# Two-block transformer kernel: the masks of the attention scores added by one fp32r product of 256 columns a head instead of two fp32 products of 128

## The chip, the cores and the metric

The kernel runs on one core of a Trainium2 chip. The metric is the device time of that core in microseconds (us): the median of three runs for the kernel before. A core has five engines that run their own instruction streams and meet only at semaphores: TensorE (PE, matrix products into PSUM), VectorE (DVE), ScalarE (ACT), GpSimd (POOL) and SyncE (SP, which here only issues transfers). A product on PE is two instructions in the trace: the load of the stationary operand (LDWEIGHTS, shown as engine PEld) and the product itself (MATMUL, engine PE). A product of fp32 operands is recorded as two such pairs, one of fp32r operands as one pair.

## The reference, cut to what matters

Two models follow each other on one sequence of 256 tokens of width 1024. The first has two layers; each layer projects the tokens, splits the result over four mixers (MoBA, MLA, stick-breaking, Mamba-2), adds the mixed heads through `w_out`, and ends in a convolved gated feed-forward. The second has four layers, which the change does not touch. All is fp32.

Three of the four mixers of a layer need a mask on a 256x256 table of scores per head, four heads each:

```
# MoBA (one block of 256) and MLA: softmax over the keys up to the query
s = einsum("bqhd,bkhd->bhqk", q, k) * scale
s = where(kpos <= qpos, s, -inf);  p = softmax(s)
# stick-breaking: strictly earlier keys
z = einsum("bqhd,bkhd->bhqk", q, k) * scale
strict = kpos < qpos
log_1mb = where(strict, log_sigmoid(-z), 0)
a = where(strict, exp(log_sigmoid(z) + reverse_cumsum(log_1mb) - log_1mb), 0)
```

With queries and keys in blocks of 128 a head has three blocks of scores that matter; two of them lie on the diagonal and take the mask, the third is whole. 12 heads a layer over 2 layers make 24 heads with two masked blocks each.

## The kernel before, in words

**Precision.** Every large product (weights times features) is taken apart into fp32r halves: a weight chunk lands in `raw` by DMA (1 MB each, issued by SP at L499), ACT writes its high part `whi` (`split`, ACT at L1171), DVE its low part `wlo` (L1658), and PE does three fp32r products per tile (L677 to L679 in the projection of the first model, L723 to L725 and L792 elsewhere). A ring of five slots holds the chunks; a slot's next transfer waits for `chunk_done`, which PE signals when it has used the chunk five back. The small products of the mixers are fp32, as they are.

**The mixers.** `Tensor.mix` (called once a layer) is PE's program, written out by hand: it weaves the projection's chunks, `chunk(0)` to `chunk(10)`, with the small products of the mixers, so that ACT and DVE can work on one mixer while PE multiplies weights. The places in it that matter here, in order: `stick_scores(0)`, `chunk(6)`, `stick_scores(1)` (after waiting for `expo`, which DVE signals at L2205), the transposes at L998, `stick_tail(0)`, `chunk(7)`, `turn_mla(0)`, `stick_tail(1)`, `chunk(8)`, `turn_mla(1)`, `chunk(9)`, `causal_scores("mla", 0)`, transposes at L1026, `causal_scores("mla", 1)`, `chunk(10)`, `causal_scores("moba", 0)` and `("moba", 1)`, the Gram products at L1042 and L1043, and then the value products up to the output projection at L792. ACT and DVE have matching programs named `mix`, also in a fixed order.

**The scores.** `stick_scores(k)` does two heads, `causal_scores(kind, i, bank)` two heads. Each head has a bank of PSUM with 384 columns: block (0,0) in columns 0:128, and the row of the second query block. In `stick_scores` the layout is (0,0), (0,1), (1,1) with the transposed scores, so its two masked blocks are columns 0:128 and 256:384; in `causal_scores` it is (0,0), (1,0), (1,1), masked at the same places. A head is four fp32 products: one of 128 columns, one of 256, and two of 128 in which the identity multiplies a table of zeros and -1e30 from `consts` (`strict_add`, `causal`) and adds it to the block. Stick-breaking and MoBA heads are 64 wide, so query and key occupy 64 partitions (the even head partitions 0:64, the odd head 64:128) and their products use 64 rows of the array; MLA heads are 96 wide and use 96. The mask products use all 128. The trace names a tensor by the memory it lies in: `sb_t` and `moba_t` appear as `xn`, `mla_t` as `proj`.

**DVE before the first mixers.** In layer 0 DVE computes the rotary angles (L1676 to L1708) and builds a bias table (`extend_bias`, L1668) between two weight splits, after waiting for `tables_in`, the transfer that brings the masks among other constants.

Of the kernel before, what the change touches and what calls it, by code (L numbers as in the profile page):

```python
# [26 lines left out]
F32R = mybir.dt.float32r  # L27
# [4 lines left out]
P = 128  # L32
SEQ, D, FF = 256, 1024, 2816
# [41 lines left out]
def constants():  # L75

    parts, at = [], 0

    def add(name, a):
        nonlocal at  # L80
        a = np.asarray(a, np.float32)
        parts.append(a)
        CONST[name] = (at, at + a.shape[1])
        at += a.shape[1]

    r, c = np.arange(P)[:, None], np.arange(P)[None, :]
    add("ident", r == c)
    add("minus_half", np.full((P, 24), -0.5))
    for name, dim in (("inv64", HD), ("inv32", ROPE)):
        inv = np.float32(1) / (np.float32(THETA) ** (np.arange(0, dim, 2, dtype=np.float32) / np.float32(dim)))  # L90
        add(name, np.broadcast_to(inv.astype(np.float32), (P, dim // 2)))
    add("upto", r <= c)
    add("ones", np.ones((P, P)))
    add("causal", np.where(c <= r, 0, BIG))
    add("upto_add", np.where(r <= c, 0, BIG))
    add("strict_add", np.where(r < c, 0, BIG))
    add("from_neg", -(r >= c).astype(np.float32))
    add("ones_neg", -np.ones((P, P)))
    add("dist", -np.abs(np.arange(P)[:, None] + np.arange(SEQ)[None, :] - 127))
    return np.concatenate(parts, 1)  # L100
# [25 lines left out]
class Semaphores:  # L126


    def __init__(self, new):
        self.params_in = new("params_in")  # L130
        self.tables_in = new("tables_in")
        self.rows_in = new("rows_in")
        self.rows_cleared = new("rows_cleared")
        self.rows_turned = new("rows_turned")
# [140 lines left out]
def view(t, **k):  # L275
    return t.rearrange("p (a b) -> p a b", **k)
# [314 lines left out]
class Tensor(Program):  # L591
# [342 lines left out]
    def mix(self, l):  # L934

        e, m, s = self.e, self.m, self.s
        ps, proj, ident = m.ps, m.proj, m.ident
        r = self.round("mixers")
# [13 lines left out]
        for t in range(TT):  # L952
            e.transpose(ps[:, 2, t * P:(t + 1) * P], m.cn[:, t, 0:P], ident)
            e.transpose(ps[0:64, 2, 256 + t * P:256 + (t + 1) * P], m.cn[:, t, P:QR], ident)
            ins = e.transpose(ps[:, 3, t * P:(t + 1) * P], m.cn[:, t, QR:QR + KVR], ident)
# [12 lines left out]
        for x in range(2):  # L968
            for j in range(2):
                for t in range(TT):  # L970
                    col = C_SB + x * GROUP + j * P
                    ins = e.transpose(ps[:, 2 + x, j * 256 + t * P:j * 256 + (t + 1) * P], proj[:, t, col:col + P], ident)
# [10 lines left out]
        for t in range(TT):  # L983
            ins = e.matmul(ps[:, 6, t * 4:t * 4 + 4], m.upto, m.a[:, t, :], start=True, stop=True)
        ins.then_inc(s.cum_done, 1)

        e.wait_ge(s.sb_kept, r)
        self.stick_scores(0)
        chunk(6)

# [96 lines left out]
    def stick_scores(self, k):  # L1087

        e, m = self.e, self.m
        for h in (2 * k, 2 * k + 1):  # L1090
            part, out = slice(64 * (h % 2), 64 * (h % 2) + 64), m.ps[:, 2 + 4 * k + h % 2, :]
            e.matmul(out[:, 0:SEQ], m.sb_t[part, 2 + h // 2, 0:P], m.sb_t[part, h // 2, :], start=True, stop=True)
            e.matmul(out[:, 0:P], m.ident, m.cst("strict_add"), start=False, stop=True, skip_group_check=True)
            e.matmul(out[:, SEQ:SEQ + P], m.sb_t[part, 2 + h // 2, P:SEQ], m.sb_t[part, h // 2, P:SEQ], start=False, stop=True,
                     skip_group_check=True)
            ins = e.matmul(out[:, SEQ:SEQ + P], m.ident, m.cst("strict_add"), start=False, stop=True, skip_group_check=True)
        ins.then_inc(self.s.z_done, 1)

    def stick_tail(self, k):

# [17 lines left out]
    def causal_scores(self, kind, i, bank):  # L1118

        e, m = self.e, self.m  # L1120
        q, k, _ = m.heads[kind]
        for h in range(2):
            out = m.ps[:, bank + h, :]
            e.matmul(out[:, 0:P], q(i, h, 0), k(i, h, 1), start=True, stop=False)
            e.matmul(out[:, 0:P], m.ident, m.cst("causal"), start=False, stop=True)
            e.matmul(out[:, P:3 * P], q(i, h, 1), k(i, h, 2), start=True, stop=True)
            ins = e.matmul(out[:, 2 * P:3 * P], m.ident, m.cst("causal"), start=False, stop=True, skip_group_check=True)
        ins.then_inc(self.s.scores, 1)

    def turn_pair(self, n, bank):  # L1130
# [512 lines left out]
class Vector(Program):  # L1643
# [488 lines left out]
    def mix(self, l):  # L2132
# [41 lines left out]
        if l == 0:  # L2174
            self.rotary_angles()
            e.wait_ge(s.tables_in, 16)
            self.extend_bias()
        self.split(5, 0)

# [462 lines left out]
def build(nc, d):  # L2642
    with ExitStack() as ctx:
        m = Memory()

        def sb(stack, name, shape, dt=F32):
            return stack.enter_context(nc.sbuf_tensor(name, shape, dt))
# [4 lines left out]
        m.xn = sb(ctx, "xn", [P, TT, D])  # L2652
        m.consts = sb(ctx, "consts", [P, CONST["dist"][0]])
        m.cols = sb(ctx, "cols", [P, ROW_TILES * P])
        m.trig = sb(ctx, "trig", [P, 192])
        m.ss = sb(ctx, "ss", [P, 2])
        m.ms = sb(ctx, "ms", [P, 2])
# [4 lines left out]
        m.rs2 = sb(ctx, "rs2", [P, 2])  # L2662
        m.st = sb(ctx, "st", [P, 60])
        m.lam_d = sb(ctx, "lam_d", [P, 4])
        m.ahead = sb(ctx, "ahead", [P, 4])
        m.pos = sb(ctx, "pos", [P, 2])
        m.pos_i = sb(ctx, "pos_i", [P, 2], I32)
        m.negmax = sb(ctx, "negmax", [P, 4, 2, 2])
# [76 lines left out]
        m.ident = m.consts[:, CONST["ident"][0]:CONST["ident"][1]]  # L2745
        m.upto = m.consts[:, CONST["upto"][0]:CONST["upto"][1]]
        m.ones = m.consts[:, CONST["ones"][0]:CONST["ones"][1]]
        m.cst = lambda n: m.consts[:, CONST[n][0]:CONST[n][1]]
        m.wide_ = lambda n: m.wide[:, WIDE[n][0]:WIDE[n][1]]
        m.row_loads = len(row_pieces())  # L2750
# [76 lines left out]
```

## Time and profile before

| | before |
|---|---|
| median of 3 runs | 2723.49 us (2721.34 to 2723.83) |
| profiled execution, its own time | 2722.85 us |
| its span, first to last instruction | 2721.1 us |
| mean granted TensorE clock | 0.983 of full speed |
| PE busy | 2628.8 us (97%), 18629 products |
| DVE busy | 1696.3 us (62%) |
| ACT busy | 1317.5 us (48%) |

The span is what the trace covers; 1.75 us of the execution's own time lie around it. A busy share is an average over stages with different limits, and a matmul's recorded duration contains the time it takes to come out of the array, so two products whose records overlap follow each other more closely than their durations say: what a product costs in a row of products is the distance between starts. The stages that the change touches are the mixers of the two layers of the first model, at about 64 to 138 us and 408 to 482 us of the span.

### The profile page before, as it was taken

The numbers are of one execution on the slowest core, as the hardware profiler recorded it, in microseconds if no ns is written. First come the engines' busy times: TensorE is split into PE (matmuls) and PEld (weight loads), VectorE is DVE, ScalarE is ACT, GpSimd is POOL, SyncE is SP. The second block draws the span as 40 slices with busy tenths as digits, with TensorE's granted clock in tenths as the row PEclk, the third lists the DMA queues.
The fourth block names the chain that finished last, engine by engine and source line by source line (L and its number), as shares of the span: only waits on it lengthen the run. The fifth ranks groups of instructions, "written<-read, shape, count | busy, mean of one in ns | idle before, by whom it ended". The sixth has DMA issues, their size and how long they took to land.

```text
span 2721.1 us, 43386 instructions
## 1 busy us (share of the span) xinstructions
PE 2628.8 (97%) x18629; PEld 2440.0 (90%) x18629; DVE 1696.3 (62%) x2201; ACT 1317.5 (48%) x1932; POOL 150.7 (6%) x228
## 2 busy tenths in 40 slices
PE   7989999999999999999998999999889999999999
PEld 7979889898998889989988998998879899888997
DVE  5668657686665656647656665655766566565763
ACT  5746457465443445445444544444454454344542
POOL 2010001000000100000010000001010000010000
PEclk9999999999999999999999999999999999998999
DMA  7256542475765637657654766765356566562763
GB/s 209 80 142 187 189 146 94 124 186 186 188 191 171 194 93 194 186 172 204 190 190 136 209 186 180 194 191 183 119 134 187 188 182 189 179 194 94 193 187 124
DMA packets 568280, 460.19 MB, mean 169 GB/s; under 512 B 12314, under 2 KB 529258, under 8 KB 568090
## 3 DMA queue, kind: packets, MB, share of 16 engines
q1 hardware_dynamic: 562643, 441.88, 55.7%
q0 software_dynamic: 4656, 15.30, 1.9%
q8 instruction: 147, 2.41, 0.4%
q10 hardware_dynamic: 791, 0.25, 0.1%
q14 instruction: 43, 0.35, 0.0%
HBM read 456.30 MB, written 1.10 MB: 168 GB/s over the span
## 4 chain that ended last, share of the span: by engine, by line
PE 87%; DVE 4%; DMA 3%; ACT 3%; issue 1%; POOL 1%; SPq 0%; DVEq 0%; POOLq 0%; ACTq 0%
PE ps L792 27%; PE ps L723 15%; PE ps L724 15%; PE ps L725 15%; PE ps L677 3%; PE ps L679 3%; PE ps L678 3%; PE ps L619 1%; DMA raw<-in_a_w_qkv 1%; ACT whi L1171 1%; DVE wlo L1658 1%; ACT h_hi L1171 1%; DMA raw<-in_w_in 1%; DMA raw<-in_ffn_w_in 1%; DVE h_lo L1719 1%
## 5 line engine op out<-in xcount | busy, mean ns | idle before, releaser
L1658 DVE TENSOR_TENSOR wlo<-raw,whi 128x2048 fp32r<-128x2048 f32 (+1 forms) x420 | 958.9, 2285 | 532.2 <-ACT whi L1171 531.5
L1171 ACT ACTIVATE whi<-raw 128x2048 fp32r<-128x2048 f32 (+1 forms) x420 | 802.0, 1914 | 807.8 <-DMA raw<-in_ff_w_in 428.8
L723 PE MATMUL ps<-h_hi,whi 128*128 128x256 f32 x3648 | 1031.5, 283 | 3.7 <-DVE h_lo L1719 3.7
L725 PE MATMUL ps<-h_hi,wlo 128*128 128x256 f32 x3648 | 1025.3, 281 | 0.0
L724 PE MATMUL ps<-h_lo,whi 128*128 128x256 f32 x3648 | 1024.8, 281 | 0.0
L723 PEld LDWEIGHTS ps<-h_hi,whi 128*128 128x128 f32 x3648 | 696.4, 191 | 10.2 <-issue 10.2
L724 PEld LDWEIGHTS ps<-h_lo,whi 128*128 128x128 f32 x3648 | 691.1, 189 | 0.0
L725 PEld LDWEIGHTS ps<-h_hi,wlo 128*128 128x128 f32 x3648 | 689.2, 189 | 0.0
L792 PE MATMUL ps<-whi,hid_lo 128*128 128x512 f32 x880 | 296.7, 396 | 0.0
L792 PE MATMUL ps<-wlo,hid_hi 128*128 128x512 f32 x880 | 295.6, 395 | 0.0
L792 PE MATMUL ps<-whi,hid_hi 128*128 128x512 f32 x880 | 294.5, 394 | 0.0
L677 PE MATMUL ps<-whi,h_hi 128*128 128x256 f32 (+1 forms) x928 | 268.4, 289 | 9.6 <-DVE wlo L1658 3.9
L679 PE MATMUL ps<-whi,h_lo 128*128 128x256 f32 (+1 forms) x928 | 263.0, 283 | 0.0
L678 PE MATMUL ps<-wlo,h_hi 128*128 128x256 f32 (+1 forms) x928 | 262.0, 282 | 0.0
L792 PEld LDWEIGHTS ps<-whi,hid_lo 128*128 128x128 f32 x880 | 165.5, 188 | 38.7
L792 PEld LDWEIGHTS ps<-whi,hid_hi 128*128 128x128 f32 x880 | 164.8, 188 | 38.7
L792 PEld LDWEIGHTS ps<-wlo,hid_hi 128*128 128x128 f32 x880 | 165.2, 188 | 37.9
L1930 DVE TENSOR_TENSOR u<-ps,rb 128x512 f32<-128x512 f32 x160 | 110.6, 691 | 139.2 <-PE ps L725 138.4
L677 PEld LDWEIGHTS ps<-whi,h_hi 128*128 128x128 f32 x928 | 177.2, 191 | 15.4 <-DVE wlo L1658 5.8
L678 PEld LDWEIGHTS ps<-wlo,h_hi 128*128 128x128 f32 x928 | 177.8, 192 | 0.6
L679 PEld LDWEIGHTS ps<-whi,h_lo 128*128 128x128 f32 x928 | 177.6, 191 | 0.0
L2417 POOL TENSOR_TENSOR ms<-ss 128x1 f32<-128x1 f32 x28 | 13.5, 484 | 1660.3 <-ACT junk L1171 1660.3
(299 smaller groups left out, 2310.2 us busy)
## 6 DMA issues: line engine op xcount, KB each, us to landing
raw<-in_ff_w_in SPq DMA_DIRECT2D x176, 1024.0 KB, 6.2
raw<-in_ff_w_out SPq DMA_DIRECT2D x88, 1024.0 KB, 4.9
raw<-in_ffn_w_in SPq DMA_DIRECT2D x44, 1024.0 KB, 6.2
raw<-in_a_w_qkv SPq DMA_DIRECT2D x24, 1024.0 KB, 5.2
raw<-in_ffn_w_out SPq DMA_DIRECT2D x22, 1024.0 KB, 5.0
raw<-in_w_in SPq DMA_DIRECT2D x20, 1024.0 KB, 5.4
raw<-in_c_w_qkv SPq DMA_DIRECT2D x12, 1024.0 KB, 5.3
raw<-in_w_out SPq DMA_DIRECT2D x8, 1024.0 KB, 4.9
```

Of the source, the lines that this page charges most:

```text
L619: ins = e.transpose(m.ps[:, 4 + n, k * P:(k + 1) * P], a[:, t, f * P:(f + 1) * P], m.ident)
L677: e.matmul(out, hi, w_hi, start=(k == 0), stop=False)
L678: e.matmul(out, hi, w_lo, start=False, stop=False)
L679: self.last = e.matmul(out, lo, w_hi, start=False, stop=(k == KT - 1))
L723: e.matmul(out, hi, m.h_hi[:, k, :], start=(k == 0), stop=False)
L724: e.matmul(out, hi, m.h_lo[:, k, :], start=False, stop=False)
L725: ins = e.matmul(out, lo, m.h_hi[:, k, :], start=False, stop=(k == KT - 1))
L792: self.last = e.matmul(m.ps[:, base + 2 * t + h, :], x, w[:, k, h * 512:(h + 1) * 512], start=(first and k == 0 and n == 0), stop=(last an ...
L1171: return self.nc.scalar.activation(*a, **k)
L1658: self.e.tensor_tensor(chunk_view(m.wlo[:, slot, :], c), chunk_view(m.raw[:, slot, :], c), chunk_view(m.whi[:, slot, :], c).bitcast(F32), ...
L1719: ins = e.scalar_tensor_tensor(m.h_lo[:, f, tok], ps[:, k, :], m.cols[:, gain + f:gain + f + 1], m.h_hi[:, f, tok].bitcast(F32), ALU.mult, ...
L1930: e.tensor_tensor(m.u[:, b % RING, :, :], view(bank, a=2), m.rb[:, :].unsqueeze(1).to_broadcast([P, 2, SEQ]), ALU.mult).then_inc(s.bank_fr ...
```

## The change

Three tables (the identity and the two masks) are copied once into fp32r (`masks`, by DVE in layer 0), and a head's two mask products become one: the fp32r identity times the fp32r mask, read twice in a row as a moving operand of 2x128 columns, into columns 0:128 and 256:384 of the bank. It comes after both score products of the head. To leave room for `masks`, `minus_half` shrinks from 24 to 16 columns and `ahead` shares the memory of `lam_d`. PE waits once for the copies (`masks_made`).

```diff
     r, c = np.arange(P)[:, None], np.arange(P)[None, :]
     add("ident", r == c)
-    add("minus_half", np.full((P, 24), -0.5))
+    add("minus_half", np.full((P, 16), -0.5))
...
         e.wait_ge(s.sb_kept, r)
+        if r == 1:
+            e.wait_ge(s.masks_made, 1)
         self.stick_scores(0)
         chunk(6)
...
             e.matmul(out[:, 0:SEQ], m.sb_t[part, 2 + h // 2, 0:P], m.sb_t[part, h // 2, :], start=True, stop=True)
-            e.matmul(out[:, 0:P], m.ident, m.cst("strict_add"), start=False, stop=True, skip_group_check=True)
             e.matmul(out[:, SEQ:SEQ + P], m.sb_t[part, 2 + h // 2, P:SEQ], m.sb_t[part, h // 2, P:SEQ], start=False, stop=True,
                      skip_group_check=True)
-            ins = e.matmul(out[:, SEQ:SEQ + P], m.ident, m.cst("strict_add"), start=False, stop=True, skip_group_check=True)
+            ins = self.add_mask(out, m.strict_r)
         ins.then_inc(self.s.z_done, 1)
+
+    def add_mask(self, out, mask):
+
+        return self.e.matmul(view(out, a=2)[:, :, 0:P], self.m.ident_r, mask.unsqueeze(1).to_broadcast([P, 2, P]), start=False, stop=True,
+                             skip_group_check=True)
...
             out = m.ps[:, bank + h, :]
-            e.matmul(out[:, 0:P], q(i, h, 0), k(i, h, 1), start=True, stop=False)
-            e.matmul(out[:, 0:P], m.ident, m.cst("causal"), start=False, stop=True)
-            e.matmul(out[:, P:3 * P], q(i, h, 1), k(i, h, 2), start=True, stop=True)
-            ins = e.matmul(out[:, 2 * P:3 * P], m.ident, m.cst("causal"), start=False, stop=True, skip_group_check=True)
+            e.matmul(out[:, 0:P], q(i, h, 0), k(i, h, 1), start=True, stop=True)
+            e.matmul(out[:, P:3 * P], q(i, h, 1), k(i, h, 2), start=False, stop=True, skip_group_check=True)
+            ins = self.add_mask(out, m.causal_r)
         ins.then_inc(self.s.scores, 1)
...
             e.wait_ge(s.tables_in, 16)
+            for i, name in enumerate(("ident", "causal", "strict_add")):
+                ins = e.tensor_copy(m.masks[:, i, :], m.cst(name))
+            ins.then_inc(s.masks_made, 1)
             self.extend_bias()
...
+        m.masks = sb(ctx, "masks", [P, 3, P], F32R)
...
-        m.ahead = sb(ctx, "ahead", [P, 4])
+        m.ahead = m.lam_d
...
+        m.ident_r, m.causal_r, m.strict_r = (m.masks[:, i, :] for i in range(3))
```

How PE's instructions stand, first the two heads of `stick_scores(1)` in a layer, before. Each row is one product, with the line that issues it, output and inputs by the memory's name, and partitions and columns of the output.

```order
L1092 MATMUL ps<-xn 128x256
L1093 MATMUL ps<-consts 128x128
L1094 MATMUL ps<-xn 128x128
L1096 MATMUL ps<-consts 128x128
L1092 MATMUL ps<-xn 128x256
L1093 MATMUL ps<-consts 128x128
L1094 MATMUL ps<-xn 128x128
L1096 MATMUL ps<-consts 128x128
```

The same two heads in the changed kernel, whose line numbers are a few higher (L1095 is the former L1092, L1096 the former L1094, L1103 the new mask product).

```order
L1095 MATMUL ps<-xn 128x256
L1096 MATMUL ps<-xn 128x128
L1103 MATMUL ps<-masks 128x2x128
L1095 MATMUL ps<-xn 128x256
L1096 MATMUL ps<-xn 128x128
L1103 MATMUL ps<-masks 128x2x128
```

Products of 64 rows and of 128 rows alternated four times a head before; now two products on the same 64 rows stand next to each other. The second place on PE is `causal_scores("mla", 0)` with the transposes behind it, before:

```order
L1124 MATMUL ps<-proj 128x128
L1125 MATMUL ps<-consts 128x128
L1126 MATMUL ps<-proj 128x256
L1127 MATMUL ps<-consts 128x128
L1124 MATMUL ps<-proj 128x128
L1125 MATMUL ps<-consts 128x128
L1126 MATMUL ps<-proj 128x256
L1127 MATMUL ps<-consts 128x128
L1026 MATMUL ps<-consts,xn 128x128 x8
```

And in the changed kernel (L1131 and L1132 are the score products, L1029 the transposes):

```order
L1131 MATMUL ps<-proj 128x128
L1132 MATMUL ps<-proj 128x256
L1103 MATMUL ps<-masks 128x2x128
L1131 MATMUL ps<-proj 128x128
L1132 MATMUL ps<-proj 128x256
L1103 MATMUL ps<-masks 128x2x128
L1029 MATMUL ps<-consts,xn 128x128 x8
```

The MoBA heads stand the same way with `xn` in place of `proj`. Nothing else on PE moved. The third place is DVE in layer 0, in the changed kernel, between the last rotary operations and the next two weight splits:

```order
L1710 TENSOR_SCALAR z<-z 128x64
L1710 TENSOR_SCALAR z<-z 128x32
L1714 TENSOR_SCALAR z<-z 128x192
L2184 CAST masks<-consts 128x128 x3
L1674 TENSOR_SCALAR z<-consts,z 32x127
L1664 TENSOR_TENSOR wlo<-raw,whi 128x2048
L2190 TENSOR_REDUCE st<-rope_tmp 128x16
```

The three casts are the only new instructions of DVE; the rest of its program is in its old order.

## Rows read from the trace of the kernel before

**Rows 1.** The page: busy time by engine, then the chain by engine.

```profile
PE 2628.8 (97%) x18629; PEld 2440.0 (90%) x18629; DVE 1696.3 (62%) x2201; ACT 1317.5 (48%) x1932; POOL 150.7 (6%) x228
...
PE 87%; DVE 4%; DMA 3%; ACT 3%; issue 1%; POOL 1%; SPq 0%; DVEq 0%; POOLq 0%; ACTq 0%
```

**Rows 2.** Timeline of PE (start, duration, engine, line), a stick-breaking pair, then `chunk(6)`.

```profile
66.13 0.70 PE L1092 MATMUL ps<-xn 64*128 64x256 f32 x2
66.76 0.49 PE L1093 MATMUL ps<-consts 128*128 128x128 f32 x2
67.18 0.49 PE L1094 MATMUL ps<-xn 64*128 64x128 f32 x2
67.59 0.49 PE L1096 MATMUL ps<-consts 128*128 128x128 f32 x2
68.01 0.70 PE L1092 MATMUL ps<-xn 64*128 64x256 f32 x2
...
69.92 0.28 PE L678 MATMUL ps<-wlo,h_hi 128*128 128x256 f32 x1
70.04 0.28 PE L679 MATMUL ps<-whi,h_lo 128*128 128x256 f32 x1
```

**Rows 3.** The same view, one MLA head and the start of the next.

```profile
102.93 0.39 PE L1124 MATMUL ps<-proj 96*128 96x128 f32 x2
...
103.37 0.60 PE L1126 MATMUL ps<-proj 96*128 96x256 f32 x2
103.81 0.39 PE L1127 MATMUL ps<-consts 128*128 128x128 f32 x2
104.03 0.39 PE L1124 MATMUL ps<-proj 96*128 96x128 f32 x2
```

**Rows 4.** The same view, the start of two MoBA heads in a row.

```profile
114.01 0.49 PE L1124 MATMUL ps<-xn 64*128 64x128 f32 x2
...
115.89 0.48 PE L1124 MATMUL ps<-xn 64*128 64x128 f32 x2
```

**Rows 5.** The same view, the four Gram products and the transposes behind them.

```profile
121.52 0.71 PE L1042 MATMUL ps<-xc 64*128 64x256 f32 x4
122.06 0.40 PE L1043 MATMUL ps<-xc 64*128 64x128 f32 x4
122.38 0.66 PE L1049 MATMUL ps<-consts,xc 128*128 128x128 f32 x4
```

**Rows 6.** The same view, fp32r products of 100 columns in layer 0.

```profile
26.33 0.28 PE L677 MATMUL ps<-whi,h_hi 128*128 128x100 f32 x1
26.45 0.27 PE L678 MATMUL ps<-wlo,h_hi 128*128 128x100 f32 x1
```

**Rows 7.** The same view, PE's only wait inside the mixers before 137 us.

```profile
88.88 0.70 PE L1104 MATMUL ps<-z,consts 128*128 128x256 f32 x2 [0.25 <-DVE z L2304]
```

**Rows 8.** Timeline of DVE in layer 0, with the idle time before an instruction.

```profile
60.64 1.75 DVE L2181 TENSOR_REDUCE st<-rope_tmp 128x16 f32<-128x1536 f32 x1 [4.07 <-ACT rope_tmp L1171]
...
73.52 0.34 DVE L2203 TENSOR_SCALAR z<-ps,neg 128x128 f32<-128x128 f32 x1
73.78 0.34 DVE L2204 SCALAR_TENSOR_TENSOR z<-ps,neg,consts 128x128 f32<-128x128 f32 x1
...
76.96 2.29 DVE L1658 TENSOR_TENSOR wlo<-raw,whi 128x2048 fp32r<-128x2048 f32 x1 [0.84 <-ACT whi L1171]
81.45 1.38 DVE L2217 TENSOR_SCALAR xc<-xt,cols 128x256 f32<-128x256 f32 x4 [2.20 <-ACT xt L1171]
```

**Rows 9.** Timeline of ACT in layer 0.

```profile
79.46 0.81 ACT L1171 ACTIVATE z<-ps 128x768 f32<-128x768 f32 x1 [1.81 <-PE ps L1096]
...
118.93 0.37 ACT L1171 ACTIVATE prob<-ps,negmax 128x128 f32<-128x128 f32 x1 [3.97 <-DVE negmax L2311]
```

**Rows 10.** Waits of SP's queue, 60 to 200 us: total, times, longest.

```profile
SPq L499 <- PE ps L679: 59.3, 6, 11.7
```

**Rows 11.** Timeline of PE, where `stick_scores(1)` starts in layer 0.

```profile
75.60 0.69 PE L1092 MATMUL ps<-xn 64*128 64x256 f32 x2
```

More of the change, by code:

```diff
@@ L131, in __init__ @@
         self.tables_in = new("tables_in")
+        self.masks_made = new("masks_made")
         self.rows_in = new("rows_in")
```

## The prediction

> **What bounds the kernel now.** I first read the page: PE is busy in 97% of the span, and the chain that ended last runs through PE for 87% of it [rows 1]. A share over the whole span does not say that the mixers are bound by PE, so I then read PE's timeline there. Between 66 and 137 us of layer 0 PE has one wait, 0.25 us before L1104 at 88.88 us, for a result of DVE [rows 7]; layer 1 repeats the pattern 344 us later. Everything else in the stage follows PE without a gap. ACT and DVE on the other hand stand still until the scores come: ACT idles 1.81 us before the second stick-breaking pair and 3.97 us before the exponentials of the first MoBA pair, the latter through DVE, which waits for the scores [rows 9]. The transfers do not run by a clock of their own either: SP's queue spends 59.3 us of this stretch, in six waits, on the projection's products [rows 10]. So the reader is to see a stage where a shorter PE program moves the others along, unless one of them is caught up with.
>
> **What a product costs.** I take distances between starts. In an MLA head (96 rows) two fp32 products of 128 columns take 103.37 - 102.93 = 0.44 us, 0.22 each, one of 256 columns 103.81 - 103.37 = 0.44, and the whole head 104.03 - 102.93 = 1.10 [rows 3]. In a stick-breaking head the same sizes take longer: 0.63 for 256 columns (66.13 to 66.76), 0.42, 0.41 and 0.42 for the three of 128, 1.88 in all [rows 2]; a MoBA head 115.89 - 114.01 = 1.88 too [rows 4]. Each of the four costs some 0.20 us more than in MLA, whether it has 128 or 256 columns. What differs is that the score products use 64 rows of the array and the mask products 128, in turn: the load of the next stationary operand is not hidden across such a change, and the 0.20 belongs to the change, not to the size. An fp32r product of 256 columns costs 70.04 - 69.92 = 0.12 [rows 2].
>
> **Do two neighbours on the same 64 rows also pay 0.20?** That is new in the changed kernel. The Gram products answer it: two groups, each a product of 256 and one of 128 columns on the same 64 rows, the groups on opposite halves of the array. All four take 122.38 - 121.52 = 0.86 us [rows 5]. One group alone streams 0.44 + 0.22 = 0.66, and with one change of 0.20 that is 0.86: the groups run beside each other, and inside a group nothing is paid between the two products. Bounds: 0 and 0.20 us; I take 0, the Gram's own row.
>
> The loads of the fp32r stream are 0.19 us long while the products stand 0.12 apart, on the same 128 rows, so loads do overlap products there [rows 2]. The Trainium skill, "TensorE: Matmul & The Clock Gate", part 3 under "What overlaps and what doesn't", says that a weight load overlaps a running product only when its row group differs. This trace disagrees for 128 rows. By that rule the two score products that now touch would still pay, which is rival B.
>
> **The mask product.** fp32r, identity stationary, 2x128 columns of a repeated table, written to two separate ranges. No row shows this shape. From below: an fp32r product of 100 columns costs 0.12 (26.33 to 26.45), as much as one of 256 [rows 6], so it cannot be much cheaper than 0.12, 0.11 at the least. From above: fp32's pace for 256 columns, 0.44 [rows 3]. I take 0.12: same type, same number of columns; the halves are longer than the 100 columns which run at that distance.
>
> **The sum.**
> - Stick-breaking and MoBA, 8 heads a layer, 16 in all. Before 1.88. After: 0.44 + 0.22 + 0.12 = 0.78, and two changes of rows instead of four, 2 x 0.20 = 0.40, together 1.18. Saved 0.70 a head, 11.2 us.
> - MLA, 4 heads a layer, 8 in all. Before 1.10, after 0.44 + 0.22 + 0.12 = 0.78. Saved 0.32 a head, 2.6 us.
> - PE in all: 13.8 us, 6.9 a layer.
> - DVE's three casts: a 128x128 operation there follows the last by 73.78 - 73.52 = 0.26 us, so 0.8 us; between 0.4 (half the price) and 1.0 (0.34 each). They stand before the split that ends before 60.64, where DVE idles 4.07 us [rows 8], and that hides them. Without the idle time 0.8 us would be added once. The casts' input is waited for at that place already; queued behind them are the bias table and a weight split used two chunks and more later. PE's new wait is fulfilled before that split even begins, at 60.64 - 2.29 = 58.3 at the latest, and is reached at 66.13; behind it stand only `stick_scores(0)` and `chunk(6)`.
>
> **Does the gain reach the end of the stage?** The first two pairs must be followed in time, as there other engines are near.
> - `stick_scores(0)` ends 1.4 us earlier, so PE reaches `stick_scores(1)` at 75.60 - 1.40 = 74.20 [rows 11]. It waits for `expo`, which DVE gives after L2204: 73.78 + 0.34 = 74.12 [rows 8]. It just fits; the casts do not move it, as DVE idled before 60.64. Between 0 and 0.1 us is lost a layer.
> - The second pair gives 1.4 more, so ACT gets its scores at 79.46 - 2.8 = 76.66 [rows 9]. What is late next would be the long run of convolutions on DVE, at 81.45, which ends in the result that PE waits for at 88.88. It waited 2.20 us for ACT; before it DVE ends a weight split at 76.96 + 2.29 = 79.25 [rows 8]. That split waited for ACT as well, which had its input from the first pair and moves by 1.4, to an end at 77.85. The convolutions can start at 81.45 - 2.8 = 78.65, so 0.8 us of room is left. Had the split not moved at all, the convolutions would start at 79.3 and 0.6 us a layer would be lost. The 0.25 us wait moves along.
> - From there on each step hangs on scores or on a chunk. MLA takes off 4 x 0.32 = 1.3 and MoBA 4 x 0.70 = 2.8. After the MoBA scores, ACT and DVE do the same work behind the same event, so the waits near 137 us keep their size and everything starts 6.9 us earlier. The next weight chunk is asked for when the output projection has used one, which is PE's doing, so it moves too.
> - The product count must fall to 18629 - 96 + 24 = 18557 (an fp32 product is recorded twice).
>
> Against its own time the profiled execution goes from 2722.85 to 2709.0 us; it lay 0.64 below the median, which so goes from 2723.49 to 2709.7. I lose 0.1 to the `expo` wait as the middle of its bounds over two layers and write 2709.8. A measurement of this kernel tells about 0.2%, 5.4 us, from no change.
>
> **Rivals.**
> - **A, the mask product at fp32's pace.** If the repeated operand or the split output range runs at 0.44, MLA saves nothing (1.10 again) and the others 1.88 - 1.50 = 0.38 a head: 6.1 us, 2717.4. For it: no row has the shape. Against: 100 and 256 columns alike take 0.12.
> - **B, the change of rows that stays.** If two products on the same 64 rows pay 0.20 as well, 16 x 0.20 = 3.2 us fewer are saved: 2713.0. Against it stand the Gram's 0.86 us, which would be 1.06.
> - **C, DVE or ACT catches up.** If `expo` or the split before the convolutions comes late, the 1.4 us of the first pair or of the second is lost in each layer: 2.8 us, 2712.6. For it: 0.08 us of room at `expo`. Against: 0.8 us at the other.
> - **D, given back in the output projection.** If the chunks behind the mixers come when they came before, the 6.9 us a layer turn into a wait there and the time stays 2723.5. Against: SP waits for PE, not for a transfer.
> - **E, slower.** Tensors declared after `masks` lie some 1.5 KB further on (three tables of 512 bytes a partition, less what the two cuts give back). If products or transfers run worse from the new places, the price falls on the whole span: the gain is eaten from 13.8 us / 18629 records = 0.74 ns a record on [rows 1], and at 1 ns the time is 2709.8 + 18.6 = 2728.4. For it only that nearly all products read moved memory; against it, L678, whose weights (`wlo`) move, and L679, whose weights (`whi`, declared before `masks`) do not, both take 0.28 us [rows 2].
>
> **How the numbers follow.** Forecast 0.71, A 0.06, B 0.11, C 0.05, D 0.04, E 0.03. The forecast's own range is 2707.5 to 2712, from 1 to 2 us for what runs differ by (2721.34 to 2723.83 before). For 8 in 10 I reach over C and B to 2716.5, and down to 2706.5 in case the exchange of rows costs a little more than 0.20 or the mask a little less. A, D and E stay out with 0.13, and some 0.03 below. Forecast, A, B and C are faster by more than 0.2%: 0.93. D is 0.04 and E 0.03.
>
> **What the changed profile would show.** The mask product's distance to the next start: 0.12 in an MLA head, 0.32 before a product of 64 rows; 0.44 or more would be A. The two score products of a stick-breaking head 0.44 apart (the load of the first aside), 0.64 would be B. The head as a whole 1.18 and 0.78. PE's wait before `stick_scores(1)` absent or under 0.1, and the 0.25 before L1104 no larger, otherwise C. The output projection starts 6.9 us earlier in layer 0 and 13.8 in layer 1; the wait behind it larger would be D. The mean distance of L723 to L725 unchanged, otherwise E. The prediction is wrong if PE's saving is there and the end does not move with it, or if a head costs more than 1.4 us.

## The result and the profile after

The changed kernel takes 2706.01 us (median of 4 runs, 2704.72 to 2706.83), the kernel before 2723.66 (2721.34 to 2724.67): a ratio of 0.9935, with a 95% interval of 0.9922 to 0.9947, 17.7 us faster. Predicted were 2709.8 us and a range from 2706.5 to 2716.5. The way and most of the size were right; the time lies half a microsecond below the range, and 3.8 below the forecast.

First the page of the changed kernel, which answers to [rows 1]: busy time by engine, and the chain by engine.

```profile
PE 2612.1 (97%) x18557; PEld 2428.2 (90%) x18557; DVE 1695.4 (63%) x2204; ACT 1317.5 (49%) x1932; POOL 150.1 (6%) x228
...
PE 88%; DVE 4%; ACT 3%; DMA 3%; issue 1%; POOL 1%; ACTq 0%; DVEq 0%; POOLq 0%
```

The count of products is the 18557 of the prediction. Lines have moved: L1095 and L1096 are the score products of stick-breaking, L1131 and L1132 those of the softmax mixers, L1103 is the mask product. PE's timeline of the stick-breaking pair, which answers to [rows 2]:

```profile
66.74 0.70 PE L1095 MATMUL ps<-xn 64*128 64x256 f32 x2
67.27 0.38 PE L1096 MATMUL ps<-xn 64*128 64x128 f32 x2
67.58 0.39 PE L1103 MATMUL ps<-masks 128*128 128x256 f32 x1
67.90 0.70 PE L1095 MATMUL ps<-xn 64*128 64x256 f32 x2
```

A head takes 67.90 - 66.74 = 1.16 us where it took 1.88. An MLA head, against [rows 3]:

```profile
100.69 0.39 PE L1131 MATMUL ps<-proj 96*128 96x128 f32 x2
100.91 0.60 PE L1132 MATMUL ps<-proj 96*128 96x256 f32 x2
101.16 0.47 PE L1103 MATMUL ps<-masks 128*128 128x256 f32 x1
101.46 0.39 PE L1131 MATMUL ps<-proj 96*128 96x128 f32 x2
```

0.77 us in place of 1.10. The mask product adds 0.77 - 0.66 = 0.11 us. Two MoBA heads start 111.57 - 110.40 = 1.17 us apart, against 1.88 in [rows 4]. PE's waits in and behind the mixers of layer 0, against [rows 7]:

```profile
86.63 0.70 PE L1111 MATMUL ps<-z,consts 128*128 128x256 f32 x2 [0.30 <-DVE z L2313]
130.52 0.66 PE L1163 MATMUL ps<-consts,xn 128*128 128x128 f32 x4 [0.31 <-DVE xn L2292]
131.71 0.70 PE L793 MATMUL ps<-whi,h_hi 128*128 128x512 f32 x2 [0.54 <-DVE h_lo L2370]
```

The wait of 0.25 us is now 0.30, and there is none before the second pair, which starts at 74.77. DVE's casts and the idle time that hides them, against [rows 8]:

```profile
55.07 0.49 DVE L2184 CAST masks<-consts 128x128 fp32r<-128x128 f32 x3
...
61.25 1.75 DVE L2190 TENSOR_REDUCE st<-rope_tmp 128x16 f32<-128x1536 f32 x1 [3.31 <-ACT rope_tmp L1177]
```

The three together take 0.49 us, not 0.8.

To see where the time went I cut the span at two places that every kernel here has: the first score product of the stick-breaking mixer, and the first product of the output projection (66.13 and 138.19 us of layer 0 in the kernel before). The "stage" is what lies between them in one layer, the "rest" what follows the second one of layer 1 up to the last product. Beside it stands the time from the start of an fp32r product to the start of the next, by line, as a mean over all of the trace's products in streams at full clock: L723, L724, L725 of the kernel before (256 columns, in the second model and the feed-forwards), the sum of these three, the sum of L677 to L679, and L792 (512 columns).

```
kernel               stage, layer 0 / 1 (us)   rest (us)   L723   L724   L725  three  L677-9   L792 (ns)
before                   72.05 / 72.11          2231.5    118.23 116.77 118.33 353.33  353.77  232.25
changed                  64.98 / 64.98          2225.5    117.04 117.71 117.62 352.37  352.86  232.30
```

The stages give 7.07 and 7.13 us, 14.2 in all, against the 13.8 of the sum. The remaining 3.5 us or so of the medians come from outside the mixers: three products of a stream take 0.96 ns less, which over 3648 of them makes 3.5 us, and 0.91 ns over 928 makes 0.8. The prediction had no term for that. The two profiled executions differ a little otherwise than the medians: the rest is 6.0 us shorter, and 2.1 us of it are given back ahead of the first stage (0.6) and between the stages (1.5).

### The profile page after: what moved, and what is told of

It reads as the page before. It is cut to its first block, busy times and chain, and to the rows that moved or that the text cites. A ratio compares the mean times of both kernels' runs of the same rounds, so it can differ in the third digit from the quotient of the medians.

```text
span 2702.9 us, 43245 instructions
## 1 busy us (share of the span) xinstructions
PE 2612.1 (97%) x18557; PEld 2428.2 (90%) x18557; DVE 1695.4 (63%) x2204; ACT 1317.5 (49%) x1932; POOL 150.1 (6%) x228
## 4 chain that ended last, share of the span: by engine, by line
PE 88%; DVE 4%; ACT 3%; DMA 3%; issue 1%; POOL 1%; ACTq 0%; DVEq 0%; POOLq 0%
PE ps L793 27%; PE ps L724 15%; PE ps L726 15%; PE ps L725 15%; PE ps L678 3%; PE ps L680 3%; PE ps L679 3%; PE ps L620 1%; ACT whi L1177 1%; DMA raw<-in_a_w_qkv 1%; DVE wlo L1664 1%; ACT h_hi L1177 1%; DMA raw<-in_ffn_w_in 1%; DVE h_lo L1725 1%; ACT prob L1177 1%
## 5 line engine op out<-in xcount | busy, mean ns | idle before, releaser
L724 PE MATMUL ps<-h_hi,whi 128*128 128x256 f32 x3648 | 1028.4, 282 | 3.5 <-DVE h_lo L1725 3.5
L725 PE MATMUL ps<-h_lo,whi 128*128 128x256 f32 x3648 | 1024.1, 281 | 0.0
L724 PEld LDWEIGHTS ps<-h_hi,whi 128*128 128x128 f32 x3648 | 689.7, 189 | 10.1 <-issue 10.1
L725 PEld LDWEIGHTS ps<-h_lo,whi 128*128 128x128 f32 x3648 | 689.4, 189 | 0.0
L679 PE MATMUL ps<-wlo,h_hi 128*128 128x256 f32 (+1 forms) x928 | 263.1, 283 | 0.0
L679 PEld LDWEIGHTS ps<-wlo,h_hi 128*128 128x128 f32 x928 | 179.9, 194 | 0.6
```

The costliest lines, as they stand in the source:

```text
L679: e.matmul(out, hi, w_lo, start=False, stop=False)
L724: e.matmul(out, hi, m.h_hi[:, k, :], start=(k == 0), stop=False)
L725: e.matmul(out, hi, m.h_lo[:, k, :], start=False, stop=False)
```

## Experiments

Two theories stood after the comparison. **P**: the new table moved the large tensors in memory, and from their new places the streams of fp32r products run a little closer. **Q**: the layout does nothing, and the rest of the gain is the new products' or chance. The tensors that move are the slots `raw` and `wlo`, the features (`h_hi`, `h_lo`) and all that is allocated behind them; `whi` is allocated ahead of `masks` and stays where it was. The experiments also take the prediction's steps apart one by one. Each ran in five rounds beside the kernel before; ratios carry their 95% interval.

**1. The layout without the products.** The code of before with this edit:

```diff
-    add("minus_half", np.full((P, 24), -0.5))
+    add("minus_half", np.full((P, 16), -0.5))
+        m.masks = sb(ctx, "masks", [P, 3, P], F32R)      # never used
-        m.ahead = sb(ctx, "ahead", [P, 4])
+        m.ahead = m.lam_d
```

> The code of before with the memory layout of the changed kernel: the table of 1536 bytes is allocated and never used, minus_half has 16 columns, ahead lies in lam_d. Nothing of the computation or its order changes. Theory P (the part of the gain beyond the mixers comes from where the tensors lie): the mean distance of the fp32r products L723 to L725 falls from 117.8 to about 117.4 ns, and the time by 3.6 us, to 2720.0. Theory Q (the layout is without effect and the rest of the gain comes with the new products or by chance): the time of before within 1 us and the distances of before.

Measured: 2720.36 us, ratio 0.9984 (0.9975 to 0.9992), 4.4 us faster than before without a single instruction changed. Stage 71.96 and 71.96; distances 117.07, 117.84, 117.68, as in the changed kernel. P holds, Q falls. A stretch of the second model with the same 3031 products, at a granted clock of 1.00 from end to end in every kernel shown here, has it in plain rows, its first product and its last. First the kernel before, then this one:

```profile
1035.63 0.38 PE L677 MATMUL ps<-whi,h_hi 128*128 128x256 f32 x1 [0.19 <-DVE h_lo L1719]
...
1453.95 0.28 PE L679 MATMUL ps<-whi,h_lo 128*128 128x256 f32 x1
```

```profile
1036.27 0.38 PE L677 MATMUL ps<-whi,h_hi 128*128 128x256 f32 x1 [0.19 <-DVE h_lo L1719]
...
1453.75 0.28 PE L679 MATMUL ps<-whi,h_lo 128*128 128x256 f32 x1
```

418.32 us against 417.48; the changed kernel has 1440.33 - 1022.98 = 417.35.

**2. The changed kernel with the table allocated last.** The line `m.masks = sb(...)` moves behind `m.xc`, so `raw`, `wlo` and the features lie 64 bytes lower than before the change.

> The changed kernel with the new table allocated last, so that weights, features and hidden tensors lie only 64 bytes lower than before the change and not 1472 higher. Theory P: if the distance of 1472 bytes is what helps, the time is 3.6 us above the changed kernel, 2709.6, and the mixers keep their 14.1 us; if 64 bytes do as well, 2706.0. Theory Q: 2706.0, with product distances like those of the changed kernel.

Measured: 2706.21 us, ratio 0.9928 (0.9914 to 0.9941); stages 65.00 and 65.01; distances 117.07, 117.94, 117.74. So 1472 bytes up and 64 bytes down do much the same.

**3. Sixty-four bytes more.** The code of before with `m.pad = sb(ctx, "pad", [P, 16])` ahead of the weight slots.

> The code of before with 64 unused bytes ahead of the weight slots, so that weights, features and hidden tensors lie 64 bytes higher and all before them stays. In the changed kernel they lie 1472 = 23 x 64 bytes higher, with the new table last 64 lower; both are odd multiples of 64, and both have the short distances. Theory P1 (an odd multiple of 64 bytes is what helps): about 4 us below before, with L723 at 117.0 ns and L724 at 117.8 as in the layout-only kernel. Rival P2 (what helps is the move of the constants or of the small tensors, which stay here): the time of before, L723 at 118.2.

Measured: 2734.32 us, ratio 1.0034 (1.0021 to 1.0046), 9.4 us slower. Both guesses were wrong. The distances are 117.51, 116.51 and 121.89, 355.91 for three. The same stretch of this kernel:

```profile
1043.70 0.39 PE L677 MATMUL ps<-whi,h_hi 128*128 128x256 f32 x1 [0.18 <-DVE h_lo L1719]
...
1463.95 0.28 PE L679 MATMUL ps<-whi,h_lo 128*128 128x256 f32 x1
```

420.25 us, 1.9 more than before in less than one sixth of the span, for 64 unused bytes.

**4. A hundred and twenty-eight bytes.** The same with `[P, 32]`.

> The same with 128 unused bytes. P1: an even multiple of 64, so the time and the distances of before (353.3 ns for three products). P3 (any displacement helps, before just lay badly): 4 us below before, like 64 bytes.

Measured: 2721.36 us, ratio 0.9987 (0.9978 to 0.9995). The three products take 353.43, L677 to L679 352.45, and L792 231.21 in place of 232.25: 3216 products of it, so 3.3 us. The gain has the size of experiment 1 and another origin. That the parity of 64-byte steps decides is refuted by this experiment and the one before: the odd step was slower, and the even one did not keep the distances of before.

**5. Sixty-four bytes behind the weight slots.** The pad stands ahead of `h_hi` and `h_lo`.

> The code of before with the 64 unused bytes behind the weight slots and ahead of the features and hidden tensors: raw and wlo stay, h_hi, h_lo and all behind them move. If the place of the features counts: 4 us below before. If that of the weight slots counts: the time of before, 2724.7.

Measured: 2728.41 us, ratio 1.0012 (1.0003 to 1.0021), 3.5 us slower. Three products 353.38, L677 to L679 354.47, L792 232.90. Both the places of `raw` and `wlo` and those of the tensors behind them matter.

**6. The displacement of the large tensors alone.** The code of before with `[P, 368]`, 1472 bytes, in the place of experiment 3.

> The code of before with 1472 unused bytes ahead of the weight slots: weights, features and hidden tensors lie exactly where they lie in the changed kernel, constants and small tensors stay where they were before. If the place of the large tensors alone sets the product distances: 117.05, 117.8 and 117.7 ns for the three products of the second model, 4 us below before, 2720.5, as the layout-only kernel. If the constants or small tensors have a part in it: other distances than those.

Measured: 2721.85 us, ratio 0.9989 (0.9981 to 0.9998). Distances 117.10, 118.07, 117.79, L677 to L679 352.84. It is the pattern of the changed kernel, with L724 0.1 to 0.4 ns longer than in most others of that layout. The large tensors' addresses allow the pattern, the constants have no visible part in it.

The distances come near the times. From before to each, (change of the three x 3648 + change of L677-9 x 928 + change of L792 x 3216) against the measured difference of medians:

```
kernel                 three  L677-9    L792    worked out   measured
1 layout only         352.59  352.77  232.29      -3.5 us      -4.4
3 64 bytes            355.91  354.75  232.23     +10.3         +9.4
4 128 bytes           353.43  352.45  231.21      -4.2         -3.5
5 64 bytes, behind    353.38  354.47  232.90      +2.9         +3.5
6 1472 bytes          352.96  352.84  232.20      -2.4         -2.4
```

The agreement is closer than the method allows. The distances come from one execution of each kernel and the times are medians; of experiments 3 and 6 the profiled execution is the slowest. In experiment 3 it took 16.9 us more than the profiled one of before, of which the distances explain 10.3.

The means also hide how the products run. Every trace has ten long streams, of 302 to 346 uninterrupted groups of the three products at full clock, and in each stream the group takes one time from end to end. In the kernel before it is 353.3 ns in all ten; in the changed kernel 353.3 in six and 351.1 in four. Here are the first product of a stream and that of the group 302 further on, one stream of before, then two neighbouring ones of the changed kernel:

```profile
1048.35 0.28 PE L723 MATMUL ps<-h_hi,whi 128*128 128x256 f32 x1
1155.05 0.28 PE L723 MATMUL ps<-h_hi,whi 128*128 128x256 f32 x1
```

```profile
1035.65 0.28 PE L724 MATMUL ps<-h_hi,whi 128*128 128x256 f32 x1
1141.68 0.28 PE L724 MATMUL ps<-h_hi,whi 128*128 128x256 f32 x1
1223.81 0.28 PE L724 MATMUL ps<-h_hi,whi 128*128 128x256 f32 x1
1330.51 0.28 PE L724 MATMUL ps<-h_hi,whi 128*128 128x256 f32 x1
```

106.70 us, 106.03 and 106.70. The same count for the other kernels: three streams of ten at 351.1 in experiment 1, two in experiment 2, one in experiment 6, and between two and four in the kernels of experiments 7 to 11, whose large tensors lie as in the changed kernel (and one at 356.7 in experiment 11). None is at 351.1 in experiments 4 and 5, and in experiment 3 nine are at 355.6 and one at 360.0. So the addresses have a part in which times a stream can take, but do not fix which of them it takes: experiments 1 and 6 have the same places for the large tensors, and three streams and one. What picks the stream is open. The runs of these two kernels spread over 6 to 8 us, 2716.95 to 2723.33 and 2717.16 to 2724.80, which would fit a choice made anew in each execution; with one trace of each that is not shown.

**7. One product of 256 columns, but fp32.** In `add_mask` the fp32 identity and masks of `consts` in place of the fp32r copies.

> The changed kernel with its one mask product of 2x128 columns a head in fp32 in place of fp32r. By the step of the prediction a 64-row head costs 0.44 + 0.22 + 0.44 + 2 x 0.20 = 1.50 us and an MLA head 1.10, so 0.38 a head of 16 is left of the saving, 6.1 us, beside what the layout gives: the time is 24 x 0.32 = 7.8 us above the changed kernel, 2713.8. Rival (most of the saving comes from the type, and fewer changes of rows bring nothing): the mask stage is as long as before and the time is about 2720, that of the layout alone.

Measured: 2713.60 us, ratio 0.9962 (0.9948 to 0.9976); stages 68.70 and 68.70. Against the changed kernel a stage is 3.72 us longer, 12 heads by 0.31. The sum's step (0.44 for fp32, 0.12 for fp32r) holds, and so does the other half: with fp32 kept, merging the products and taking two changes of rows away gives 71.96 - 68.70 = 3.26 us a layer, 8 heads by 0.41, two changes of 0.20 each.

**8. fp32r masks in their old places**, two products of 128 columns a head between and behind the score products:

```diff
             e.matmul(out[:, 0:P], q(i, h, 0), k(i, h, 1), start=True, stop=True)
+            self.add_one(out[:, 0:P], m.causal_r)
             e.matmul(out[:, P:3 * P], q(i, h, 1), k(i, h, 2), start=False, stop=True, skip_group_check=True)
-            ins = self.add_mask(out, m.causal_r)
+            ins = self.add_one(out[:, 2 * P:3 * P], m.causal_r)
```

> The changed kernel with two fp32r mask products of 128 columns a head, each in its old place between the score products. Theory R (the price of 0.20 us belongs to a change between 64 and 128 rows and stays when the mask is fp32r): a 64-row head costs 0.44 + 0.22 + 2 x 0.11 + 4 x 0.20 = 1.68 us, an MLA head 0.88; against the changed kernel 16 x 0.52 + 8 x 0.11 = 9.2 us more: 2715.2. Rival (the 0.20 belonged to a product of fp32 with a mask table and its doubled load): a 64-row head costs about 1.1 and the time stays near 2706.

Measured: 2730.51 us, ratio 1.0018 (1.0007 to 1.0028). One run of eleven took 8228 us, for which the record has no cause; the ratio leaves it out, and the median without it is 2729.33. A 64-row head costs 67.30 - 65.75 = 1.55 us (from a mask product to the next product on 64 rows pass 0.26, which less the change of 0.20 leaves 0.06 and not 0.11), so the changes of rows are paid, as R said. But the time is 15 us above the expectation, and slower than before, for another reason: TensorE's clock. Stretches of its mixers, granted clock in the third figure from the right (PEclk, behind the busy times of PE, PEld, DVE, ACT and POOL):

```profile
74.00:84.00 10.00, 10.00 (x56) 8.52 (x55) 6.61 (x11) 7.92 (x10) 0.00 (x0) 0.83 0.29 107
110.00:130.00 20.00, 20.00 (x135) 17.11 (x134) 10.40 (x18) 10.92 (x33) 1.64 (x1) 0.91 0.19 53
450.00:488.00 38.00, 38.00 (x208) 34.05 (x207) 15.96 (x28) 17.25 (x49) 2.33 (x2) 0.69 0.13 38
```

The changed kernel in the same windows:

```profile
74.00:84.00 10.00, 10.00 (x74) 9.22 (x73) 8.60 (x17) 9.49 (x12) 0.00 (x0) 1.00 0.29 107
110.00:130.00 20.00, 20.00 (x161) 17.84 (x159) 12.10 (x27) 11.52 (x31) 2.57 (x3) 1.00 0.20 53
450.00:488.00 38.00, 37.15 (x237) 31.77 (x237) 24.43 (x40) 18.64 (x41) 6.14 (x4) 1.00 0.21 56
```

PE is busy all of the 10, 20 and 38 us, and part of them runs at 1.2 GHz and not at 2.4; before the clock fell PE had been working without a recorded gap on heads in which every product changes between 64 and 128 rows. In layer 1 it stayed down through the value products, and the stage grew to 79.61 us, against 71.17 in layer 0. The kernel before has the same alternation with fp32 masks and kept the full clock. The ten runs here had a mean granted clock of 0.971 to 0.978, and 20 of the 21 of before beside them 0.979 to 0.983, so the fall is not an accident of the profiled execution. "Busy" is said of the records: 0.80 us of a head's 1.55 are changes of rows, and the records cover them too.

**9. Two fp32r products of 128 columns, both behind the score products.**

> The changed kernel with two fp32r mask products of 128 columns a head, both behind the score products. From the kernel with the masks in their old places an fp32r product of 128 columns streams 0.06 us, so the head costs what it does in the changed kernel, 1.16 and 0.77. If the half-rate stretches inside the mixers come from the alternation of 64 and 128 rows: none here, 2706. If they come from fp32r products of 128 columns as such: half-rate stretches at 78 and 460 us again and about 10 us more.

Measured: 2713.82 us, ratio 0.9960 (0.9947 to 0.9972). Neither case: a head costs 68.35 - 67.14 = 1.21 us and not 1.16, the stage of layer 0 65.81 with the full clock, but in layer 1 the clock fell at the end of the MoBA scores and the stage took 70.60:

```profile
450.00:488.00 38.00, 37.15 (x223) 32.58 (x222) 20.70 (x39) 16.34 (x37) 6.14 (x4) 0.87 0.21 54
```

The head is longer because the second mask product starts 0.16 us behind the first. So a full alternation is not needed for the clock to fall: with two short products in place of one of 256 it fell in one of two layers of the one profiled execution, and no other kernel here but that of experiment 8 shows a fall inside the mixers. The five runs had 0.977 to 0.981, against 0.980 to 0.982 in the changed kernel, and spread over 7 us, so in some executions it may not fall at all. By the medians one product with 256 columns is worth 7.8 us over two with 128 (7.2 if each is first set against the runs of before beside it), of which the products themselves explain 2 x (65.81 - 64.98) = 1.7.

**10. Both heads' score products first, then both masks.**

```diff
         for h in (2 * k, 2 * k + 1):
             ...
-            ins = self.add_mask(out, m.strict_r)
+        for h in range(2):
+            ins = self.add_mask(m.ps[:, 2 + 4 * k + h, :], m.strict_r)
```

and in the same way in `causal_scores`.

> The changed kernel, but the score products of both heads of a pair come first and both masks after them. The even head's products use rows 0 to 63, the odd head's 64 to 127. If the two heads then run beside each other as the Gram products do (0.86 us for four products) a pair of 64-row heads costs 0.86 + 0.12 + 0.12 + 0.20 = 1.30 us in place of 2.32, 8 such pairs in two layers, 8.2 us saved: 2697.8. If opposite halves do not overlap here, a pair still changes rows twice and not four times: 2 x 0.66 + 0.24 + 0.40 = 1.96, 2.9 us saved: 2703.1. MLA pairs (96 rows) keep 1.54 either way. If the exchange of rows cost nothing, 2706.0.

Measured: 2699.74 us, ratio 0.9904 (0.9890 to 0.9917). PE's timeline, a pair and the start of the next chunk:

```profile
67.18 0.71 PE L1095 MATMUL ps<-xn 64*128 64x256 f32 x4
67.72 0.40 PE L1096 MATMUL ps<-xn 64*128 64x128 f32 x4
68.04 0.50 PE L1104 MATMUL ps<-masks 128*128 128x256 f32 x2
68.38 0.28 PE L678 MATMUL ps<-whi,h_hi 128*128 128x256 f32 x1
```

Four score products in 0.86 us, as the Gram products in [rows 5], and a pair up to the next chunk in 1.20, where the changed kernel has 68.97 - 66.74 = 2.23: the halves do run beside each other. Four pairs of 1.03 would make 4.1, but the stage is 61.89, 3.09 shorter, since DVE's `expo` is now late by the difference:

```profile
75.22 0.71 PE L1095 MATMUL ps<-xn 64*128 64x256 f32 x4 [1.03 <-DVE z L2215]
```

That is the mechanism of the prediction's rival C, one step further on.

**11. The same, with `expo` given earlier.** On DVE the scaling of the MLA queries and keys moves behind the block that signals `expo`.

> The kernel with both heads' score products first, and on DVE the scaling of the MLA queries and keys (1.76 us) behind the block that gives expo instead of ahead of it. PE's wait of 1.03 us before the second stick-breaking pair should go in both layers, as expo comes 1.8 us earlier; PE asks for the scaled tensor 9 us later only. 2.0 us less than that kernel: 2697.7. If the wait's time only returns at the 0.30 us wait for the convolutions' result: no change, 2699.7.

Measured: 2698.45 us, ratio 0.9908 (0.9893 to 0.9923), not to be told from experiment 10. The wait before the second pair is gone, and most of it came back at the next one, for the end of the convolutions:

```profile
82.33 0.70 PE L1112 MATMUL ps<-z,consts 128*128 128x256 f32 x2 [0.91 <-DVE z L2314]
```

Stage 61.42 and 61.42, 0.47 less where 1.03 had been waited. The second expectation describes it, though not wholly. DVE's chain from the scores to there now bounds the stage's first half. Experiment 10 and this one are the fastest kernels of the study, 25 and 26 us below before.

## Why the prediction was right and where it failed

- **PE bounds the stage and the others follow.** Right. The stage shrank by 7.1 us a layer, PE has no new wait, and the waits at L1104 and near 137 us kept their size (0.25 to 0.30, 0.31 to 0.31).
- **The price of a change of rows, 0.20 us, and none between neighbours on the same 64 rows.** Right. The head came to 1.16 where 1.18 was worked out. Rival B's 1.38 is out, and with it, for this case, the rule of the Trainium skill ("TensorE: Matmul & The Clock Gate", part 3, "What overlaps and what doesn't") that the prediction set beside it: the second product's load was hidden on equal rows. Experiment 7 shows the two changes alone at 0.41 a head.
- **The mask product at 0.12.** Right, 0.11. Rival A is out; experiment 7 is A's price made real, 7.6 us against the expected 7.7.
- **The casts are hidden.** Right, and smaller: 0.49 us, with DVE's idle time down from 4.07 to 3.31.
- **`expo` just fits.** Right for the changed kernel; DVE's last operation of it ended at 74.72, 0.05 us before PE's product at 74.77, and in experiment 10 PE had to wait.
- **Given back in the output projection (D).** No, the 6.9 us a layer did not turn into a wait there. Between the stages 1.5 us more passed in the profiled execution, and the rows behind the projection of layer 0, first before and then changed, show a longer wait, and transposes that took 1.97 us and not 1.09, at a granted clock of 0.50 (155.93 to 157.80 us) and not 1.00 (161.37 to 162.40); behind layer 1 the wait was 3.74 against 0.21 + 3.37.

```profile
161.37 1.09 PE L619 MATMUL ps<-consts,xn 128*128 128x128 f32 x8 [3.97 <-DVE xn L1770]
```

```profile
155.93 1.97 PE L620 MATMUL ps<-consts,xn 128*128 128x128 f32 x8 [4.88 <-DVE xn L1776]
```

- **The failed step: the new places of the tensors, entered at zero.** The prediction named them only in rival E, as a way to become slower, with a chance of 0.03, and argued from two durations of 0.28 us that they would not matter. A duration rounded to 10 ns cannot show what decides here, a shift of 0.3 ns a product over 14,000 products. That mean hides two values besides: four long streams of ten run at 351.1 ns a group of three, and six at the 353.3 of before. The effect was there, with the other sign: 4.4 us in experiment 1 (2.2 to 6.8 by its interval), and it could as well have been 9.4 the other way, as experiment 3 shows for 64 bytes. 14.2 from the stages and 4.4 from the layout make 18.6, against 17.7 measured. That the time came within half a microsecond of the range is in part luck, since the sign of the missing term was not to be foreseen. With a term of plus or minus 5 the range would have held.

What stays open is the rule by which an address sets the distance, and what picks the streams that run closer. Parity of 64-byte steps is refuted by experiments 3 and 4; `raw` and `wlo` and the tensors behind them both have a part; five new layouts are too few for more.

## What to carry to other kernels

Where small fp32 products alternate between 64 and 128 rows of the array, count the changes before the columns: each cost 0.20 us here, as much as an fp32 product of 128 columns, and ordering them by rows, with the two halves of the array side by side, gave more than the type did: 2 x 3.26 us in experiment 7 and 2 x 3.09 in experiment 10, against 2 x 3.72 for the type. An edit that allocates a tensor is two edits: run its layout alone, with the old code, before the gain is booked on the products, and run it often, as its effect can differ from run to run. And in experiments 8 and 9 a shorter PE program came with a lower clock; look at the granted clock of the stage, not only at gaps.

## What the runs showed of the hardware

- The place of `raw`, `wlo`, the features and what lies behind them in SBUF, moved by 64 to 1472 bytes, changed the mean distance of fp32r products of 256 columns by line between 116.5 and 121.9 ns and a kernel's time by -4.4 to +9.4 us, with the same instructions. A long stream keeps one time for three products from end to end: 353.3 ns in the kernel before, 353.3 or 351.1 in the changed kernel, 355.6 or 360.0 with 64 bytes more.
- The granted clock fell to 1.2 GHz while PE was busy without a gap: 0.83 over 10 us, 0.91 over 20 and 0.69 over 38 in experiment 8. The Trainium skill, "TensorE: Matmul & The Clock Gate", under "HAM oscillation — how this bites in real kernels", puts such falls down to idle gaps between bursts of products; here no row before the fall shows a gap, so recorded gaps do not explain it. What in the mix of products let it fall these runs do not say.
- An estimate from experiment 8: an fp32r product of 128 columns between products on other rows streams in about 0.06 us (0.26 less the 0.20 of the change), half the 0.11 of one with 256. Directly behind each other two of them stand 0.16 apart (67.99 to 68.15 us in experiment 9), and the 100-column products of [rows 6] 0.12, each with new weights.
